# Three modulation blocks accumulated on VectorE instead of TensorE, and two blocks moved to the NSA attention units

## The chip, the cores and the metric

One NeuronCore of a Trainium2 chip runs the whole program; the other cores are idle. The metric is the device time of one launch in microseconds (us), the median over runs. TensorE (PE in the profile) multiplies matrices, VectorE (DVE) and ScalarE (ACT) work elementwise, GpSimd is POOL, and SyncE (SP) issues the transfers from HBM into the on-chip SBUF. Each engine runs its own instructions strictly in order and waits on semaphores for the others. Matrix products land in eight banks of PSUM.

## What is computed

The reference is one layer with three mixers and a mixture of experts, followed by two layers (NSA attention, then a recurrent mixer), each with a SwiGLU feed-forward part. T = 256 tokens, D = 1024, everything in float32. The part that the change touches is the modulation: a vector times a weight matrix of 1024 x 6144, three times over, whose results shift, scale and gate the activations.

```python
def first_block(x, c, ctx, c_ctx, w_mod, b_mod, ...):
    sc = jax.nn.silu(c)
    mod_x = (sc @ w_mod[layer] + b_mod[layer]).reshape(-1, N_MOD, d)
    mod_c = (scc @ w_mod[layer][:, :n_mod_c * d] + ...)      # n_mod_c = 2
    hx = modulate(rms_norm(x, g_mix[layer]), mod_x[:, 0], mod_x[:, 1])
    ...
    x = x + mod_x[:, 2, None] * mx
    hx = modulate(rms_norm(x, g_ffn[layer]), mod_x[:, 3], mod_x[:, 4])
    x = x + mod_x[:, 5, None] * expert_choice_ffn(hx, ...)

def second_block(x, c, ada_w, ada_b, ...):
    cond = jax.nn.silu(c)
    for layer in range(DEPTH_2):
        mod = (cond @ ada_w[layer] + ada_b[layer])[:, None, :]
        sh1, sc1, g1, sh2, sc2, g2 = jnp.split(mod, 6, axis=-1)
```

## The kernel before

**One list of steps.** `plan_steps` writes one list, `STEPS`, and every engine walks it in order and executes its share of each step: `("kr", 0)` is 96 matmuls on PE and two copies out of PSUM on ACT, `("rot", "kr", 0)` one matmul on PE and three operations on DVE. So the place of a step in the list fixes its place in each engine's queue.

**Weights as chunks.** All weights come as 408 chunks of 128 x 2048 float32 (1 MB), in the order in which the steps use them (`CHUNKS`). SP loads them into the slots of `ring`. In the first stage there are six slots (0, 1, 2, 3, 6, 8), from `("gate", 0)` on four (0 to 3), for the experts twelve, and afterwards nine. SP loads chunk c into its slot only when the semaphore `chunk_used` says that the chunk six places earlier has been used. PE raises it: a finished step adds to `owed`, and the next plain matmul hands `owed` over (`settle`). In the first gate stage SP takes the chunks in order too, so that gate 1 queues behind gate 0.

**Split.** A projection weight is used as a pair of fp32r numbers. `("split", x)` makes it: ACT copies the chunk to an upper slot (4 or 5) as the high part (L1240), then DVE subtracts to leave the low part in the chunk's own slot (L1540). PE then does three matmuls of 256 columns for each product (`mm3`), waiting once for `lo_ready`. Each split stands in the list one projection ahead of its use.

**Modulation.** The modulation rows are nine blocks of 2048 columns, each of eight chunks `("mod", b, k)`. For a chunk PE does four matmuls (one per 32 output rows of `mods`, PSUM bank 7) of 512 columns with the vector `silu_c` as weights, accumulating over k. `("mod_row", b)` copies the rows out on ACT (L1329), and `("mod_out", b)` transposes them on PE (L622) and adds the bias on DVE (L1585, L1588). Block 0 comes first, since its results are needed by `("apply", 0)`, which normalizes the inputs and splits them (L1530, L1525 on DVE; L1224, L1226 on ACT). Blocks 1 to 5 are `fill`: seven items before the first projection (`FILL_START`), then two or one after a projection (`FILL_LONG`, `FILL_SHORT`), and one for each unit of window and neighbourhood attention (`att_s`, `att_n`, `att_t`, `att_o`). Blocks 6 to 8 are the fill of the 37 rounds of NSA units (`nsa_s`, `nsa_n`, `nsa_t`, `nsa_o`). Block 1 is first used when the mixers' output is added to x, block 2 in the norm ahead of the experts, block 3 in the norm ahead of the NSA part, blocks 4 and 5 from that part's output on.

**Order of the stages.** Block 0 and the norm; the projections kr, qr, vr, gr, kvw, qw, kn, vn, qn with retention between them; gates; window and neighbourhood attention; branches and merge; the experts; the NSA projections, compression and units; feed-forward; the recurrent mixer; feed-forward.

Of the kernel before, what the change touches and what calls it, by code (L numbers as in the profile page):

```python
# [20 lines left out]
ALU = mybir.AluOpType  # L21
# [20 lines left out]
MOD_BLOCKS, LAST_BLOCKS = 9, 6  # L42
# [6 lines left out]
FILL_START, FILL_LONG, FILL_SHORT, GATE_EVERY = 7, 2, 1, 2  # L49
# [27 lines left out]
def plan_steps():  # L77
# [10 lines left out]
    fill = blocks(1, LAST_BLOCKS)  # L88

    def take(n):  # L90
        for _ in range(min(n, len(fill))):
            s.append(fill.pop(0))

    s.append(("apply", 0))
    take(FILL_START)
# [41 lines left out]
    fill += blocks(LAST_BLOCKS, MOD_BLOCKS)  # L137
    for i in range(units + LAG + 2):
        if i < units:
            s.append(("nsa_s", i))  # L140
        take(1)
        if 0 <= i - LAG + 1 < units:
            s.append(("nsa_n", i - LAG + 1))
        if 0 <= i - LAG < units:
            s.append(("nsa_t", i - LAG))
        if 0 <= i - LAG - 1 < units and (i - LAG - 1) % 2:
            s.append(("nsa_o", (i - LAG - 1) // 2))
# [80 lines left out]
def with_splits(steps):  # L228
# [4 lines left out]
    for u in uses:  # L233
# [10 lines left out]
        before.setdefault(x, []).append(("split", u))  # L244
    return [y for x in steps for y in before.get(x, []) + [x]], place
# [89 lines left out]
def build(nc, w, small, out):  # L335
# [9 lines left out]
    with ctx:  # L345
# [63 lines left out]
        decay_in = room(9216, N_DECAY)  # L409
        rope_a, rope_b = room(15872, 2, T), room(16384, 2, T)  # L410
# [66 lines left out]
        silu_ready, mod_done, sq_x, sq_ctx = sem("silu_ready"), sem("mod_done"), sem("sq_x"), sem("sq_ctx")  # L477
        sq_ready, std_ready, h_scaled, h_ready = sem("sq_ready"), sem("std_ready"), sem("h_scaled"), sem("h_ready")
# [135 lines left out]
        def _(pe):  # L614
# [120 lines left out]
            def step_mod(blk, k):  # L735

                ck = ring[:, slot_of(CHUNK_NO[("mod", blk, k)]), :]
# [721 lines left out]
        def _(dve):  # L1459
# [117 lines left out]

            def step_mod_out(blk):
# [16 lines left out]
                elif blk == 2:  # L1595
                    link(v.scalar_tensor_tensor(mod_a[:, 1, :], mod[:, 32:40, 0], 1.0, gain_of(1), ALU.add, ALU.mult))
                elif blk in (LAST_BLOCKS - 1, MOD_BLOCKS - 1):

                    for ni in (3, 4) if blk == LAST_BLOCKS - 1 else (5, 6):
                        at = SHIFT2[ni] + 8  # L1600
                        link(v.scalar_tensor_tensor(mod_a[:, ni, :], mod2[:, at:at + 8], 1.0, gain_of(ni), ALU.add,
                                                    ALU.mult))
# [358 lines left out]
            def step_rnn_add():  # L1961
                for p in range(4):
# [3 lines left out]
                     "mod_out": step_mod_out,  # L1966
# [181 lines left out]
```

## Time and profile before

| | us |
|---|---|
| median of 3 runs (1866.33 to 1878.32) | 1867.08 |
| span of the profiled execution | 1866.7 |
| PE busy (86% of the span) | 1601.3 |
| DVE busy (44%) | 814.8 |
| ACT busy (31%) | 585.5 |
| bytes read from HBM | 435 MB, 234 GB/s over the span |

The kernel has stages with different limits. In slices 12 to 21 of the page's 40 (about 560 to 1010 us) the transfers run at 421 to 423 GB/s, which are the experts; elsewhere PE is 80 to 100% busy and the transfers run at half that rate or less. A share of busy time averages over these stages, so a change in one of them has to be read from that stage alone.

### The profile page before, as it was taken

Reading aid. Unit: us, or ns where it says so; the run is one execution under the profiler, and the core shown is the slowest. Engines: PE = TensorE matmul, PEld = TensorE weight load, DVE = VectorE, ACT = ScalarE, POOL = GpSimd, SP = SyncE. Lnnn points to the kernel's source line nnn. Section 1 sums busy time; section 2 is a strip of 40 time slices with the busy share of each in tenths; the row PEclk is TensorE's granted clock in tenths of the full one; section 3 lists DMA queues with packets and bytes.
Section 4 is the critical chain, followed back from the end, with each engine's and each line's share of the span. In section 5 each row is a group of like instructions: output and inputs, shape, how many; then the busy total and the mean of one; then the engine's idle time right before and its main releaser. Section 6 shows DMA issues by size and latency. Waiting matters only on the chain. (4 is left out here: it accounts for less than half of the span.)

```text
span 1866.7 us, 27285 instructions
## 1 busy us (share of the span) xinstructions
PE 1601.3 (86%) x11234; PEld 1176.9 (63%) x11234; DVE 814.8 (44%) x1274; ACT 585.5 (31%) x833; POOL 20.6 (1%) x21
## 2 busy tenths in 40 slices
PE   5899998999966666766667799999999989889999
PEld 1689886666941111111114787547899989779999
DVE  4433336576641101000011765455665466766553
ACT  3322135663320000000001431443433344833332
POOL 0000020000000000000000000000000000200000
PEclk9899999999977667677767896989999999989999
DMA  9665455511729999999999253752455435335550
GB/s 395 252 253 204 181 183 211 237 68 46 284 104 423 421 422 422 421 422 422 423 422 421 77 182 111 254 197 99 143 186 182 181 136 181 136 113 183 182 178 24
DMA packets 60418, 437.76 MB, mean 235 GB/s; under 512 B 6720, under 2 KB 6848, under 8 KB 7456
## 3 DMA queue, kind: packets, MB, share of 16 engines
q1 hardware_dynamic: 59328, 428.89, 58.8%
q10 hardware_dynamic: 720, 4.94, 0.6%
q0 software_dynamic: 272, 2.49, 0.4%
q8 instruction: 77, 1.26, 0.3%
q14 instruction: 21, 0.17, 0.0%
HBM read 435.25 MB, written 1.05 MB: 234 GB/s over the span
## 5 line engine op out<-in xcount | busy, mean ns | idle before, releaser
L618 PE MATMUL bank<-H_r,ring_r 128*128 128x256 f32 x3488 | 509.8, 288 | 18.5 <-DVE H_r L1525 18.5
L618 PEld LDWEIGHTS bank<-H_r,ring_r 128*128 128x128 f32 x3488 | 464.5, 196 | 24.0 <-issue 22.6
L618 PE MATMUL bank<-arena_r,ring_r 128*128 128x256 f32 x2776 | 397.6, 287 | 25.2 <-DVE ring_r L1540 22.2
L1540 DVE TENSOR_TENSOR ring_r<-ring,ring_r 128x2048 fp32r<-128x2048 f32 x136 | 314.1, 2311 | 216.4 <-ACT ring_r L1240 216.0
L618 PEld LDWEIGHTS bank<-arena_r,ring_r 128*128 128x128 f32 x2776 | 369.2, 194 | 40.2 <-issue 18.6
L1240 ACT ACTIVATE ring_r<-ring 128x2048 fp32r<-128x2048 f32 x136 | 259.6, 1909 | 218.6 <-PE bank L618 164.4
L934 PE MATMUL bank<-ring,arena 128*32 128x512 f32 x1024 | 201.8, 881 | 105.9 <-DMA ring<-in_w 104.4
L934 PEld LDWEIGHTS bank<-ring,arena 128*32 128x32 f32 x1024 | 24.6, 127 | 267.8 <-DMA ring<-in_w 259.8
L618 PE MATMUL bank<-arena 128*64 128x256 f32 (+8 forms) x664 | 172.3, 402 | 4.0 <-DVE arena L1797 2.0
L1789 DVE TENSOR_TENSOR arena<-arena,bank 64x512 f32<-64x512 f32 x16 | 11.1, 692 | 290.7 <-ACT arena L1335 290.7
L618 PEld LDWEIGHTS bank<-arena 64*128 64x128 f32 (+4 forms) x664 | 99.4, 185 | 57.5 <-issue 28.6
L1335 ACT ACTIVATE arena<-bank 64x512 f32<-64x512 f32 x16 | 9.4, 589 | 387.2 <-PE bank L934 387.2
L955 PE MATMUL bank<-ring,arena 128*32 128x256 f32 x1024 | 91.7, 514 | 21.4 <-DMA ring<-in_w 13.5
L618 PE MATMUL bank<-ring,silu_c 128*32 128x512 f32 x576 | 85.8, 685 | 25.8 <-DMA ring<-in_w 17.0
L955 PEld LDWEIGHTS bank<-ring,arena 128*32 128x32 f32 x1024 | 37.0, 141 | 71.2 <-DMA ring<-in_w 33.1
L1797 DVE COPY arena<-bank 32x256 f32 x64 | 26.9, 420 | 123.1 <-PE bank L955 122.4
L1409 ACT ACTIVATE arena<-bank 128x256 f32<-128x256 f32 x44 | 16.9, 384 | 153.7 <-PE bank L618 153.7
L618 PE MATMUL bank<-ring_r,H_r 128*128 128x256 f32 (+1 forms) x256 | 57.6, 285 | 0.0
L618 PE MATMUL bank<-ring_r 128*128 128x256 f32 (+1 forms) x304 | 56.4, 283 | 0.0
L1919 DVE TENSOR_TENSOR arena<-arena,bank 128x256 f32<-128x256 f32 x44 | 18.5, 421 | 75.7 <-ACT arena L1409 75.7
L618 PEld LDWEIGHTS bank<-ring_r 128*128 128x128 f32 x304 | 48.3, 193 | 0.0
L618 PEld LDWEIGHTS bank<-ring,silu_c 128*32 128x32 f32 x576 | 13.1, 113 | 55.1 <-DMA ring<-in_w 28.5
(233 smaller groups left out, 1274.5 us busy)
## 6 DMA issues: line engine op xcount, KB each, us to landing
ring<-in_w SPq DMA_DIRECT2D x408, 1024.0 KB, 10.4
ring<-in_bias POOLq DMA_DIRECT2D x1, 2048.0 KB, 7.8
consts<-in_consts ACTq DMA_DIRECT2D x1, 1567.0 KB, 25.2
X<-in_x ACTq DMA_DIRECT2D x1, 1024.0 KB, 10.8
arena<-in_ctx ACTq DMA_DIRECT2D x1, 1024.0 KB, 15.3
arena<-in_decay ACTq DMA_DIRECT2D x1, 1024.0 KB, 19.8
out_t<-X SPq DMA_DIRECT2D x4, 256.0 KB, 2.5
wide<-in_wide POOLq DMA_DIRECT2D x1, 256.0 KB, 9.1
```

The lines of the kernel that those rows point to most:

```text
L618: i = nc.tensor.matmul(o, lhsT, rhs, start=start, stop=stop, skip_group_check=grouped)
L934: last = mm(bank[0][32 * j:32 * j + 32, :], x_cur[:, k, :], ring[:, k, 512 * j:512 * j + 512], start=k == 0, stop=k == KT - 1)
L955: last = mm(bank[2][32 * j:32 * j + 32, 0:T], hid_t[:, k % 4, k // 4 * CAP:k // 4 * CAP + CAP], ck[:, kk, j * T:j * T + T], start=k == 0, ...
L1240: f(r(hi), lo, ACT.Copy).then_inc(hi_ready, 1)
L1335: f(silu_g[64:P, :], bank[0][0:64, :], ACT.Silu).then_inc(silu_g_ready, 1)
L1409: f(ffn_g[:, i % 2, :], b[:, 0:T], ACT.Silu).then_inc(ffn_silu, 1)
L1540: v.tensor_tensor(r(lo), lo, r(hi), ALU.subtract).then_inc(lo_ready, 1)
L1789: v.tensor_tensor(hid[64:P, :], silu_g[64:P, :], bank[0][64:P, :], ALU.mult).then_inc(hid_ready, 1)
L1797: o = v.tensor_copy(y_tok[32 * u:32 * u + 32, i, j * T:(j + 1) * T], bank[2][32 * j:32 * j + 32, 0:T])
L1919: link(v.tensor_tensor(p, ffn_g[:, i % 2, :], b[:, T:2 * T], ALU.mult))
```

## The change

Blocks 1, 2 and 3 are no longer multiplied on PE. A new step `("mod_add", b, k)` on DVE multiplies the 128 x 2048 chunk by the vector's element of each partition and adds it to `mod_acc` (2048 columns in `arena`). PE no longer reads these chunks: at `("mod", b, k)` it waits for the semaphore `mod_added`, and at k = 7 four matmuls with ones as weights sum `mod_acc` over the partitions. The chunk counts as used only after that place in PE's order. The step stands ahead of the chunk two places earlier in `CHUNKS` (`ADD_AHEAD`). `FILL_START` is gone; three items follow a long and two a short projection. Blocks 4 and 5 move to the NSA units, where each second round now takes two items.

```diff
-MOD_BLOCKS, LAST_BLOCKS = 9, 6
+MOD_BLOCKS, ADD_BLOCKS = 9, 4
-FILL_START, FILL_LONG, FILL_SHORT, GATE_EVERY = 7, 2, 1, 2
+ADD_AHEAD = 2
+
+FILL_LONG, FILL_SHORT, GATE_EVERY = 3, 2, 2
...
-    fill = blocks(1, LAST_BLOCKS)
+    fill = blocks(1, ADD_BLOCKS)
...
     s.append(("apply", 0))
-    take(FILL_START)
...
-    fill += blocks(LAST_BLOCKS, MOD_BLOCKS)
+    fill += blocks(ADD_BLOCKS, MOD_BLOCKS)
...
-        take(1)
+        take(1 + i % 2)
...
+    for c, x in enumerate(CHUNKS):
+        if x[0] == "mod" and 0 < x[1] < ADD_BLOCKS:
+            at = CHUNKS[c - ADD_AHEAD]
+            before.setdefault(("kr", 0) if at[:2] == ("mod", 0) else at, []).append(("mod_add",) + x[1:])
...
+        mod_acc = room(11264, CHUNK)
...
+        mod_added = sem("mod_added")
...
             def step_mod(blk, k):
 
+                if 0 < blk < ADD_BLOCKS:
+                    pe.wait_ge(mod_added, (blk - 1) * KT + k + 1)
+                    if k == KT - 1:
+                        begin(("mod_row", blk))
+                        for j in range(4):
+                            mm(mods[32 * j:32 * j + 32, :], ones[:, 0:32], mod_acc[:, 512 * j:512 * j + 512], True, True,
+                               mod_done if j == 3 else None)
+                    owed[0] += 1
+                    return
...
+            def step_mod_add(blk, k):
+                c = CHUNK_NO[("mod", blk, k)]
+                at = 2 * k if blk < 3 else 16 + k
+                dve.wait_ge(landed[slot_of(c)], 16 * landed_count(c))
+                if k == 0 and blk == 1:
+                    dve.wait_ge(silu_ready, 2)
+                if k == 0 and blk > 1:
+
+                    dve.wait_ge(mod_done, blk)
+                if k == 0:
+                    o = v.tensor_scalar(mod_acc, ring[:, slot_of(c), :], silu_c[:, at:at + 1], None, ALU.mult)
+                else:
+                    dve.wait_ge(mod_added, (blk - 1) * KT + k)
+                    o = v.scalar_tensor_tensor(mod_acc, ring[:, slot_of(c), :], silu_c[:, at:at + 1], mod_acc, ALU.mult,
+                                               ALU.add)
+                o.then_inc(mod_added, 1)
```

Where the new step lands shows first in VectorE's queue, from the end of `("apply", 0)` (the H_r rows) on. A row with `ring_r<-ring,ring_r` is the low half of a split. Before, six of them stand there, with one `mod_out` (L1585) between:

```order
L1525 SCALAR_TENSOR_TENSOR H_r<-H,mod,ring_r 128x256
L1540 TENSOR_TENSOR ring_r<-ring,ring_r 128x2048 x4
L1585 TENSOR_TENSOR mod<-bank,cols 128x16 x2
L1540 TENSOR_TENSOR ring_r<-ring,ring_r 128x2048 x2
L1632 COPY arena<-bank 128x2x256 x2
```

Now, at the same place (kr 1's split first; kr 0's stands ahead of `("apply", 0)`):

```order
L1541 SCALAR_TENSOR_TENSOR H_r<-H,mod,ring_r 128x256
L1556 TENSOR_TENSOR ring_r<-ring,ring_r 128x2048
L1604 TENSOR_SCALAR arena<-ring,silu_c 128x2048
L1607 SCALAR_TENSOR_TENSOR arena<-ring,silu_c,arena 128x2048 x3
L1556 TENSOR_TENSOR ring_r<-ring,ring_r 128x2048
L1607 SCALAR_TENSOR_TENSOR arena<-ring,silu_c,arena 128x2048 x3
L1556 TENSOR_TENSOR ring_r<-ring,ring_r 128x2048
L1607 SCALAR_TENSOR_TENSOR arena<-ring,silu_c,arena 128x2048
L1604 TENSOR_SCALAR arena<-ring,silu_c 128x2048
```

Four multiply-adds of 2048 columns now stand between the splits of kr 1 and qr 0, and three between those of qr 0 and qr 1. Of the latter the first two (k = 4 and 5) are waited for by PE ahead of qr 0.

On TensorE, between the last matmul of kr 1 and the first of qr 0 (with the semaphores that each waits for), two chunks of fill stood before:

```order
L618 MATMUL bank<-ring_r 128x256
L618 MATMUL bank<-ring,silu_c 32x512 [waits act_emptied,landed0]
L618 MATMUL bank<-ring,silu_c 32x512 x3
L618 MATMUL bank<-ring,silu_c 32x512 [waits landed1]
L618 MATMUL bank<-ring,silu_c 32x512 x3
L618 MATMUL bank<-arena_r,ring_r 128x256 [waits lo_ready]
```

Now nothing stands there but the wait for VectorE's sum:

```order
L625 MATMUL bank<-ring_r 128x256 x2
L625 MATMUL bank<-H_r,ring_r 128x256
L625 MATMUL bank<-ring_r 128x256
L625 MATMUL bank<-arena_r,ring_r 128x256 [waits mod_added,lo_ready]
L625 MATMUL bank<-H_r,ring_r 128x256
```

The two groups of fill are gone, and the first matmul of qr 0 waits for `mod_added` besides `lo_ready`.

The order of the chunks moves with it. Before it was mod 0 0 to mod 1 6 (numbers 0 to 14), kr 0 (15), mod 1 7 (16), kr 1 (17). Now it is mod 0 0 to 0 7 (0 to 7), kr 0 (8), mod 1 0 to 1 2 (9 to 11), kr 1 (12), mod 1 3 to 1 5 (13 to 15), qr 0 (16), mod 1 6 and 1 7 (17, 18), qr 1 (19), mod 2 0 (20), vr 0 (21), and so on to qn 1 (48) in slot 0 and gate 0 (49), in slot 0 too.

## Rows read from the trace of the kernel before

**Rows 1.** Windows of core 0: busy us (x instructions) per engine, PEclk, DMA share, GB/s

```profile
core 0: us, PE busy (x) PEld busy (x) DVE busy (x) ACT busy (x) POOL busy (x), PEclk, DMA share, GB/s
...
61.50:67.00 5.50, 5.49 (x25) 5.50 (x26) 2.29 (x1) 1.91 (x1) 0.00 (x0) 0.50 1.03 427
...
77.00:267.00 190.00, 190.00 (x1494) 169.48 (x1498) 65.86 (x65) 44.01 (x37) 7.83 (x2) 1.00 0.53 205
267.00:304.00 37.00, 29.80 (x198) 20.28 (x190) 26.36 (x23) 18.05 (x20) 1.72 (x1) 0.99 0.61 227
304.00:312.00 8.00, 7.64 (x43) 7.64 (x44) 4.15 (x8) 6.18 (x9) 0.00 (x0) 0.62 0.36 132
312.00:400.00 88.00, 87.08 (x556) 60.41 (x555) 52.55 (x112) 56.99 (x86) 0.00 (x0) 1.00 0.47 181
...
600.00:900.00 300.00, 199.28 (x1332) 42.52 (x1328) 26.69 (x60) 22.56 (x30) 0.00 (x0) 0.69 1.01 422
...
1155.00:1290.00 135.00, 129.33 (x676) 68.99 (x669) 68.54 (x179) 54.45 (x183) 0.00 (x0) 0.88 0.52 187
```

**Rows 2.** The same windows for instructions on `silu_c` alone: the modulation matmuls

```profile
61.00:267.00 206.00, 20.04 (x164) 4.02 (x168) 0.00 (x0) 0.00 (x0) 0.98 0.52 203
...
312.00:400.00 88.00, 8.52 (x64) 1.28 (x64) 0.00 (x0) 0.00 (x0) 1.00 0.47 181
1155.00:1290.00 135.00, 30.41 (x192) 3.89 (x184) 0.00 (x0) 0.00 (x0) 0.88 0.52 187
```

**Rows 3.** Timeline of PE and ACT, 49 to 63 us: start, us, instruction, [idle before <-releaser]

```profile
49.78 1.18 PE L618 MATMUL bank<-ring,silu_c 128*32 128x512 f32 x8 [2.59 <-DMA ring<-in_w]
52.27 1.93 PE L618 MATMUL bank<-ring,silu_c 128*32 128x512 f32 x8 [1.30 <-DMA ring<-in_w]
...
57.22 1.91 ACT L1240 ACTIVATE ring_r<-ring 128x2048 fp32r<-128x2048 f32 x1 [0.78 <-DMA ring<-in_w]
...
61.51 0.58 PE L618 MATMUL bank<-arena_r,ring_r 128*128 128x256 f32 x1 [4.82 <-DVE ring_r L1540]
...
62.18 1.91 ACT L1240 ACTIVATE ring_r<-ring 128x2048 fp32r<-128x2048 f32 x1 [3.05 <-DMA ring<-in_w]
```

**Rows 4.** Timeline of DVE: `("apply", 0)` first and last, splits, a scalar_tensor_tensor

```profile
44.33 0.48 DVE L1530 SCALAR_TENSOR_TENSOR H<-X,mod_a,norm_t 128x256 f32<-128x256 f32 x1
...
56.61 0.48 DVE L1525 SCALAR_TENSOR_TENSOR H_r<-H,mod,ring_r 128x256 fp32r<-128x256 f32 x1
...
59.16 2.29 DVE L1540 TENSOR_TENSOR ring_r<-ring,ring_r 128x2048 fp32r<-128x2048 f32 x1 [2.08 <-ACT ring_r L1240]
...
118.97 0.68 DVE L1614 TENSOR_TENSOR arena<-arena,consts 128x512 f32<-128x512 f32 x1
...
223.27 0.69 DVE L1648 SCALAR_TENSOR_TENSOR ring<-bank,ring 128x512 f32<-128x512 f32 x1 [1.37 <-PE bank L618]
...
315.65 0.49 DVE L1697 TENSOR_SCALAR ring<-ring,stat 128x512 f32<-128x512 f32 x1
```

**Rows 5.** Timeline: PE after vr 0, SP's load of gr 0's chunk, ACT's copy

```profile
115.28 1.92 PE L618 MATMUL bank<-ring,silu_c 128*32 128x512 f32 x16
...
116.49 2.39 SPq L538 DMA_DIRECT2D ring<-in_w  x3
...
121.30 1.92 ACT L1240 ACTIVATE ring_r<-ring 128x2048 fp32r<-128x2048 f32 x1 [15.67 <-DMA ring<-in_w]
```

**Rows 6.** Timeline of ACT: copies out of PSUM that close kr 1, kvw; DVE's closes kvw and kn 1

```profile
82.95 0.60 ACT L1258 ACTIVATE arena<-bank 128x512 f32<-128x512 f32 x1 [3.49 <-PE bank L618]
...
88.70 0.60 ACT L1258 ACTIVATE arena<-bank 128x512 f32<-128x512 f32 x1 [5.16 <-PE bank L618]
...
152.87 0.60 ACT L1266 ACTIVATE arena<-bank 128x512 f32<-128x512 f32 x1 [3.66 <-PE bank L618]
...
163.55 0.69 DVE L1637 COPY arena<-bank 128x512 f32<-128x512 f32 x1 [11.94 <-PE bank L618]
...
205.07 0.69 DVE L1641 COPY arena<-bank 128x512 f32<-128x512 f32 x1 [3.50 <-PE bank L618]
```

**Rows 7.** Timeline of PE at 304 us: the restart after a stall

```profile
304.36 0.58 PE L618 MATMUL bank<-arena_r,ring_r 128*128 128x256 f32 x1 [5.28 <-DVE ring_r L1540]
```

**Rows 8.** Timeline of PE in an NSA round

```profile
1170.89 1.06 PE L618 MATMUL bank<-ring,silu_c 128*32 128x512 f32 x8
1171.89 0.66 PE L622 MATMUL bank<-consts,arena 128*128 128x128 f32 x4
```

**Rows 9.** Waits of PE, 1155 to 1290 us: waited for, us, times, longest

```profile
PE bank L622 <- DVE arena L1903: 3.6, 2, 2.3
PE bank L618 <- DVE arena_r L1910: 1.0, 1, 1.0
```

More of the change, by code:

```diff
@@ L1596, in step_mod_out @@
                     link(v.scalar_tensor_tensor(mod_a[:, 1, :], mod[:, 32:40, 0], 1.0, gain_of(1), ALU.add, ALU.mult))
-                elif blk in (LAST_BLOCKS - 1, MOD_BLOCKS - 1):
-                    for ni in (3, 4) if blk == LAST_BLOCKS - 1 else (5, 6):
+                elif blk in (3, 5, MOD_BLOCKS - 1):
+                    for ni in {3: (3,), 5: (4,)}.get(blk, (5, 6)):
                         at = SHIFT2[ni] + 8
@@ L1965, in _ @@
             parts = {"sum_sq": step_sum_sq, "apply": step_apply, "split": step_split, "decay": step_decay,
-                     "mod_out": step_mod_out,
+                     "mod_out": step_mod_out, "mod_add": step_mod_add,
                      "rot": step_rot, "vr": values("vr", v_r), "vn": values("vn", v_n), "kvw": step_kvw, "kn": step_kn,
```

## The prediction, made before the changed kernel was run

> **What bounds the kernel now.** I read the windows first, to see which stages the change can touch. From 77 to 267 us, the stretch of the projections, PE is busy without a gap at full clock, DVE 65.9 of 190 us, the transfers at half rate [rows 1]. So PE is the bound there and a chunk of fill taken off it should count in full. In the gate stage (267 to 304) PE already idles 7 us; in the attention units to 400 it is busy 87.1 of 88; in the NSA stretch 129.3 of 135. At 600 to 900 us the transfers run at 422 GB/s and set the pace; nothing changes there, so that stage only shifts. Second, the fill itself: the modulation matmuls hold PE for 20.0 us between 61 and 267 us (164 records at eight a chunk, 20.5 chunks), 8.5 us for eight chunks up to 400, and 30.4 us for 24 chunks in the NSA units [rows 2]. Third, the start: ACT takes kr 0's chunk the moment it lands (57.22), the low part follows, PE starts at 61.51, and chunks land 2.5 us apart (49.78, 52.27) [rows 3]. Fourth, and this decides it, what happens to a weight that is loaded only when PE frees its slot: PE finishes vr 0 at 115.28, SP issues at 116.49, ACT starts on the chunk at 121.30 [rows 5]. From the freeing matmul to ACT that is 6.0 us. Then ACT needs 1.9 and DVE 2.3 before PE can start. Before, PE hides these 10.3 us behind other projections and behind fill that needs no partner.
>
> **The start.** kr 0's chunk is now the ninth instead of the sixteenth: seven times 2.5 us sooner, 57.2 - 17.5 = 39.7 us, so it no longer delays anyone. Its split stands ahead of `("apply", 0)` and pushes that by 2.3 us, to 59.2 (it ran from 44.33 to 57.0 [rows 4]). PE can follow the tiles and is left with about three quarters of kr 0 then. Half a key projection is 5.75 us (82.95 to 88.70 [rows 6]), and the restart costs 2.9 us of half clock as before (5.5 us at 0.50 [rows 1]): kr 0 ends at 59.2 - 2.9 + 11.5 + 2.9 = 70.8 instead of 61.5 + 11.5 + 2.9 = 75.9. Gain 5.
>
> **Work removed from PE up to the end of the gate stage.** 20.0 us of chunks, and three more in the gate stage that stand half in idle time: 1.5. Three sums with ones come back: four matmuls of 512 columns each, as a chunk, 1.0 us [rows 2], so 3. Sum with the start: -5 - 20 - 1.5 + 3 = -23.5.
>
> **Work added to DVE.** The multiply-add reads two tensors. No row shows it at 2048 columns. A scalar_tensor_tensor of 512 columns takes 0.69, a tensor_tensor 0.68, and the latter takes 2.29 at 2048 columns [rows 4]; I take 2.3. The lower bound, from a tensor_scalar of 512 columns (0.49), is 4 x 0.4 = 1.6. 24 x 2.3 = 55 us on DVE, which has 124 free: by its sum DVE is not the bound. The Trainium skill ("VectorE: DVE Perf Modes", the perf-mode tier table) gives tensor_scalar a faster mode on fp32 in SBUF, 1.23 us for 2048 elements; that would hold for the three first chunks alone and take 3 us off DVE.
>
> **The new loop.** PE passes a modulation chunk only after DVE has added it, DVE adds in its own order behind the splits, a split waits for a chunk, and SP loads a chunk only when PE has passed the one six places ahead. With up to three such chunks between two projections, six slots are little more than one projection deep. I walk it with: freed slot to ACT 6.0 us for the first chunk, 2.5 for each behind it (1.05 MB at 422 GB/s [rows 1]), ACT 1.9, DVE 2.3, multiply-add 2.3, half projection 5.75.
> - kr 1 runs 70.8 to 82.4. Its first matmul frees chunks 8 to 11, so 14, 15 and 16 (qr 0) are loaded: ACT at 70.8 + 6.0 + 5.0 = 81.8, low part 86.1, then the two multiply-adds that PE waits for, 90.7. PE stalls 8.3.
> - qr 0's start frees 12 to 15; qr 1 is the second to land: ACT 90.7 + 8.5 = 99.2, low part 103.5, one multiply-add 105.8. PE is done with qr 0 at about 98. Stall 7.9.
> - gr 0 waits 5.7 for low part and two multiply-adds. gr 1: gr 0 starts 146.7, gr 1's chunk is second: 155.2, 159.4, 161.8 with the add; gr 0 ends 152.4. Stall 9.4.
> - In the same way qw 1 6.3, kn 0 4.3, the last row copy 0.7. vr 0, vr 1 and kvw run 11.5 and 16.4 us (152.87 less 5.75 to 163.55 [rows 6]) and give the loop time; there it stalls little or not.
> - gate 0 has slot 0 after qn 1 itself. Its load starts when qn 1 is done, and only a 0.9 us matmul step is left to hide it: 9.5. Before, slot 0 there held a modulation chunk long passed.
>
> Sum: 8.3 + 7.9 + 5.7 + 9.4 + 6.3 + 4.3 + 0.7 + 9.5 = 52. The walk over the old order gives no stall between kr 0 and gate 0 and the end of kn 1 at 205.4; the trace has 205.07 [rows 6]. Clock: after 5.28 us of idling [rows 7] the stretch from 304 on again starts at a granted clock of half, 0.62 over 8 us [rows 1]. A restart costs up to 2.75 us; six stalls are that long, 0 to 16. Partly the slower PE only eats into the next stall; I take 10. Up to the end of the gate stage: -23.5 + 52 + 10 = +38.
>
> **Attention units.** 8.5 us of chunks and two transposing steps of 0.6 leave a stretch in which PE is 99% busy: -9.5, less if DVE and ACT (52.6 and 57.0 of 88 us) then set the pace.
>
> **NSA units.** Sixteen chunks come in, 1.0 us each from start to the next instruction [rows 8], and two transposes of 0.6: +17. They fill some of the 4.6 us that PE waits there for DVE [rows 9]. The transfers: 40 chunks x 2.5 = 100 us in some 150, still free. I take +14.
>
> **Sum.** 1866.7 + 38 - 9.5 + 14 = 1909 us (span and median of before differ by 0.4).
>
> **Rivals.**
> 1. The loads keep up (faster). This needs the chunk of the next projection to be freed at least 10.3 us before PE wants it, for the eight places above; then PE stays the bound, the stalls and the clock term vanish, and the sum is -23.5 - 9.5 + 14 = -19: 1848. For it speaks PE's 100% against DVE's 35%; against it that the slot count and order above are fixed by the code. The Trainium skill ("Perfetto Trace Analysis", Identifying the Most-Contended Engine) says to relieve the engine with the highest occupancy first, which is this rival's case. The same page (Optimization Strategy) says that a gap that repeats can mean too few buffers, which is mine.
> 2. The loop costs half (same). If the 6.0 us were 4 and the slow clock cost nothing, each of eight stalls shrinks by 2 to 3: 52 becomes about 32, and the sum 1866.7 - 23.5 + 32 - 9.5 + 14 = 1880; with multiply-adds of 1.6 the seven after the splits take 5 more off, 1875.
> 3. Worse than the walk (slower still). DVE's queue also delays the rotations and value copies, retention and the slow clock count in full (+6), the attention units do not speed up (+9.5), NSA costs 17 (+3): 1928. If, beyond this, the NSA transfers bound (40 chunks at their pace with SP waiting for slots), up to 8 more.
>
> **How the numbers follow.** About 1% is what a measurement of this kernel can tell from no change. The loop as walked has 0.70 and rival 3 0.11; both lie over 1% slower. Rival 2 has 0.12, half of it within 1% (up to 1886). Rival 1 has 0.07. So faster 0.07, same 0.06, slower 0.87. The likeliest case's own range is 1890 to 1925. The range that should hold the time is 1880 to 1930: below it stand rival 1 and part of 2, above it part of 3.
>
> **What would show it.** In the changed profile: PE idle before the first matmuls of qr 0, qr 1, gr 0, gr 1, qw 1, kn 0 and gate 0, each 4 to 10 us, released by DVE's multiply-add or its low part; PEclk at 0.5 behind them; ACT's high-part copies waiting for the transfers; PE's busy share between 77 and 300 us at 75 to 80% instead of 100. kr 0 starting before 50 us shows the start right. The multiply-add at 2.3 us shows the row used right. The modulation chunks in the NSA units at 40 x 1.0 to 1.25 us. It would be wrong if PE stays gapless through the projections, which would mean that the loads come sooner than six places behind PE, or if the attention units give back the shift.

## The result, and the profile after

The changed kernel takes 1910.5 us (median of 4 runs, 1905.7 to 1915.5) against 1866.7 us of the kernel before on the same chip: a ratio of 1.023, 95% interval 1.019 to 1.026, so it is slower by about 2%. The profiled execution has a span of 1903.9 us, 37.2 more than the 1866.7 of before. The other 6 to 7 us between the medians are spread between executions, and I explain the 37.2.

These are the windows of the changed kernel, with the columns of [rows 1]:

```profile
core 0: us, PE busy (x) PEld busy (x) DVE busy (x) ACT busy (x) POOL busy (x), PEclk, DMA share, GB/s
...
77.00:267.00 190.00, 149.44 (x1093) 139.25 (x1092) 100.31 (x78) 34.65 (x28) 0.00 (x0) 0.87 0.46 182
267.00:304.00 37.00, 25.27 (x172) 23.88 (x171) 13.96 (x8) 9.03 (x9) 9.35 (x2) 0.88 0.45 170
...
312.00:400.00 88.00, 76.59 (x480) 60.55 (x479) 58.28 (x97) 57.12 (x80) 0.00 (x0) 0.94 0.31 108
600.00:900.00 300.00, 197.69 (x1344) 43.51 (x1336) 26.66 (x60) 22.57 (x30) 0.00 (x0) 0.70 1.01 422
```

In the projections PE was busy 190 of 190 us and is now busy 149.4; DVE went from 65.9 to 100.3, the transfers from 205 to 182 GB/s. No engine is full in this stretch any more. The experts (600 to 900 us) are as before, at 422 GB/s. PE's waits from 60 to 312 us (waited for: us, times, longest) say for what it stands still:

```profile
PE bank L625 <- DVE arena L1607: 39.8, 6, 9.2
PE bank L625 <- DVE ring_r L1556: 11.7, 1, 11.7
PE bank L629 <- ACT norm_t L1345: 0.7, 1, 0.7
```

L1607 is DVE's multiply-add, L1556 the low part of a split. The same stretch of before has 12.4 us of waits, 4.8 of them the start of kr 0 and 5.3 a wait at 304 us.

I split the 37.2 us with operations on DVE that both kernels have: the second retention variance (end of the gate stage) and the first addition to X of each later part. Starts in us, before and after (the shift is cumulative, its own part is what that part of the kernel adds):

| place | before | after | shift | its own part |
|---|---|---|---|---|
| second retention variance | 288.84 | 328.00 | +39.2 | +39.2 |
| first addition of mix_out | 492.57 | 522.42 | +29.9 | attention -9.3 |
| first addition of combine | 1014.97 | 1043.66 | +28.7 | experts -1.2 |
| first addition of nsa_out | 1292.50 | 1333.37 | +40.9 | NSA +12.2 |
| last addition to X | 1863.41 | 1900.57 | +37.2 | rest -3.7 |

The experts and the rest run the same steps in both kernels; why the rest took 3.7 us less is left open.

### The profile page after: what moved, and what is told of

It reads as the page before. It is cut to its first block and busy times, and to the rows that moved or that the text cites. A ratio compares the mean times of both kernels' runs of the same rounds, so it can differ in the third digit from the quotient of the medians.

```text
span 1903.9 us, 27031 instructions
## 1 busy us (share of the span) xinstructions
PE 1577.8 (83%) x11066; PEld 1178.6 (62%) x11066; DVE 868.0 (46%) x1298; ACT 585.1 (31%) x833; POOL 20.4 (1%) x21
## 3 DMA queue, kind: packets, MB, share of 16 engines
q8 instruction: 75, 1.23, 0.3%
## 5 line engine op out<-in xcount | busy, mean ns | idle before, releaser
L625 PE MATMUL bank<-H_r,ring_r 128*128 128x256 f32 x3488 | 513.7, 289 | 18.5 <-DVE H_r L1541 18.5
L625 PE MATMUL bank<-arena_r,ring_r 128*128 128x256 f32 x2776 | 410.3, 291 | 58.1 <-DVE ring_r L1556 31.2
L625 PEld LDWEIGHTS bank<-arena_r,ring_r 128*128 128x128 f32 x2776 | 377.8, 197 | 73.5 <-issue 39.6
L1556 DVE TENSOR_TENSOR ring_r<-ring,ring_r 128x2048 fp32r<-128x2048 f32 x136 | 315.2, 2319 | 217.1 <-ACT ring_r L1256 216.7
L950 PE MATMUL bank<-ring,arena 128*32 128x512 f32 x1024 | 195.8, 858 | 108.5 <-DMA ring<-in_w 108.1
L625 PE MATMUL bank<-arena 128*64 128x256 f32 (+8 forms) x664 | 166.5, 394 | 4.0 <-DVE arena L1830 2.0
L625 PEld LDWEIGHTS bank<-arena 64*128 64x128 f32 (+4 forms) x664 | 96.7, 181 | 51.5 <-issue 23.2
L625 PE MATMUL bank<-ring,silu_c 128*32 128x512 f32 x384 | 57.2, 695 | 22.8 <-DMA ring<-in_w 12.1
L625 PE MATMUL bank<-arena,consts 128*128 128x512 f32 (+4 forms) x76 | 35.1, 765 | 34.9 <-DVE arena L1607 25.0
L1952 DVE TENSOR_TENSOR arena<-arena,bank 128x256 f32<-128x256 f32 x44 | 18.5, 421 | 74.9 <-ACT arena L1425 74.9
L1607 DVE SCALAR_TENSOR_TENSOR arena<-ring,silu_c,arena 128x2048 f32<-128x2048 f32 x21 | 49.3, 2348 | 1.6 <-DMA ring<-in_w 0.7
## 6 DMA issues: line engine op xcount, KB each, us to landing
X<-in_x ACTq DMA_DIRECT2D x1, 1024.0 KB, 10.7
```

The lines of the kernel that those rows point to most:

```text
L625: i = nc.tensor.matmul(o, lhsT, rhs, start=start, stop=stop, skip_group_check=grouped)
L950: last = mm(bank[0][32 * j:32 * j + 32, :], x_cur[:, k, :], ring[:, k, 512 * j:512 * j + 512], start=k == 0, stop=k == KT - 1)
L1556: v.tensor_tensor(r(lo), lo, r(hi), ALU.subtract).then_inc(lo_ready, 1)
L1607: o = v.scalar_tensor_tensor(mod_acc, ring[:, slot_of(c), :], silu_c[:, at:at + 1], mod_acc, ALU.mult, ALU.add)
L1952: link(v.tensor_tensor(p, ffn_g[:, i % 2, :], b[:, T:2 * T], ALU.mult))
```

## The loop, as the trace of the changed kernel shows it

Here is the stall before gr 1, from start to end. In the timeline of PE the two records at 144.08 are the rotation ahead of gr 0, which is drawn to 146.1, and I count gr 0 from there (its first record stands at 145.13, over the rotation's end); the eight records at 160.68 are the four matmuls with ones that sum block 2, and gr 1 follows them:

```profile
144.08 2.04 PE L625 MATMUL bank<-arena,consts 128*128 128x512 f32 x2 [5.00 <-DVE arena L1607]
...
160.68 1.94 PE L625 MATMUL bank<-arena,consts 128*32 128x512 f32 x8 [7.77 <-DVE arena L1607]
```

SP's loads, ACT's copy and DVE's queue in the same stretch of the timeline:

```profile
146.51 2.17 SPq L545 DMA_DIRECT2D ring<-in_w  x4
...
153.86 1.91 ACT L1256 ACTIVATE ring_r<-ring 128x2048 fp32r<-128x2048 f32 x1 [18.11 <-DMA ring<-in_w]
...
155.87 2.29 DVE L1556 TENSOR_TENSOR ring_r<-ring,ring_r 128x2048 fp32r<-128x2048 f32 x1 [7.63 <-ACT ring_r L1256]
158.08 2.34 DVE L1607 SCALAR_TENSOR_TENSOR arena<-ring,silu_c,arena 128x2048 f32<-128x2048 f32 x1
```

Read it as a chain: gr 0 starts at 146.1 and frees the slots; SP issues at 146.5; ACT has gr 1's chunk, the second to land, at 153.86 (7.7 us after the start; 8.5 in the walk); high part 1.9, low part 2.3, and then the multiply-add behind it in DVE's queue, 2.3, to 160.4. PE was done with gr 0 at 152.9. DVE itself stands idle 7.6 us in this chain, waiting for ACT, which waits for the transfer: DVE is the last link and not the bound, though its multiply-add of 2.3 us is part of the chain. The other stalls, PE's rows in order of time (qr 0, the sum and qr 1, qw 1, kn 0, mod_out 3, gate 0; gr 0 is the 5.00 above):

```profile
90.37 0.55 PE L625 MATMUL bank<-arena_r,ring_r 128*128 128x256 f32 x1 [9.22 <-DVE arena L1607]
...
105.24 1.93 PE L625 MATMUL bank<-arena,consts 128*32 128x512 f32 x8 [7.39 <-DVE arena L1607]
...
199.91 0.55 PE L625 MATMUL bank<-arena_r,ring_r 128*128 128x256 f32 x1 [5.63 <-DVE arena L1607]
...
212.06 1.19 PE L625 MATMUL bank<-arena,consts 128*128 128x256 f32 x2 [4.81 <-DVE arena L1607]
...
228.04 0.66 PE L629 MATMUL bank<-consts,norm_t 128*128 128x128 f32 x4 [0.74 <-ACT norm_t L1345]
...
302.00 0.58 PE L625 MATMUL bank<-arena_r,ring_r 128*128 128x256 f32 x1 [11.73 <-DVE ring_r L1556]
```

Every stall but the 0.74 is followed by a half clock. These windows of the changed kernel begin at six of the restarts; PEclk is the third number from the end:

```profile
90.40:93.80 3.40, 3.40 (x16) 3.40 (x17) 2.17 (x1) 0.00 (x0) 0.00 (x0) 0.50 0.44 145
105.20:111.50 6.30, 6.26 (x31) 4.63 (x32) 3.58 (x2) 1.91 (x1) 0.00 (x0) 0.55 0.50 176
144.10:148.40 4.30, 4.30 (x14) 3.27 (x15) 4.11 (x4) 0.00 (x0) 0.00 (x0) 0.50 0.20 32
160.70:165.40 4.70, 4.70 (x15) 2.01 (x16) 2.02 (x3) 1.91 (x1) 0.00 (x0) 0.50 0.31 94
...
212.10:216.60 4.50, 4.50 (x19) 4.32 (x20) 4.42 (x5) 1.92 (x1) 0.00 (x0) 0.50 0.46 126
302.00:306.00 4.00, 4.00 (x21) 4.00 (x22) 2.15 (x1) 0.00 (x0) 0.00 (x0) 0.58 0.00 0
```

Length times (1 - PEclk) is what each costs: 1.7, 2.8, 2.2, 2.4, 2.3, 1.7, and 1.5 behind qw 1 (3.6 us at 0.57): 14.5 us. The windows end a little behind the half clock where PEclk is above 0.50; PE itself ran at 0.50 for 3.1 to 5.6 us each time.

And this is what the change costs DVE, by form, 40 to 230 us (busy us, mean ns | idle before):

```profile
L1607 DVE SCALAR_TENSOR_TENSOR arena<-ring,silu_c,arena 128x2048 f32<-128x2048 f32 x21 | 49.3, 2348 | 1.6 <-DMA ring<-in_w 0.7
L1556 DVE TENSOR_TENSOR ring_r<-ring,ring_r 128x2048 fp32r<-128x2048 f32 x13 | 29.8, 2292 | 48.4 <-ACT ring_r L1256 48.3
L1604 DVE TENSOR_SCALAR arena<-ring,silu_c 128x2048 f32<-128x2048 f32 x3 | 3.9, 1285 | 4.7 <-PE bank L625 4.7
```

## The experiments

"Variance" is the start of the second retention variance: 288.84 before, 328.00 in the changed kernel. A ratio is against the kernel before on the chip of that run, where its median was 1866.0 to 1867.7 us; a time set against the changed kernel's 1910.5 us compares two chips.

### Each half of the change alone: `e1_nsa_only`, `e2_order_pe`

The first is the kernel before with blocks 4 and 5 moved to the NSA units:

```diff
-MOD_BLOCKS, LAST_BLOCKS = 9, 6
+MOD_BLOCKS, LAST_BLOCKS = 9, 4
...
-        take(1)
+        take(1 + i % 2)
```

> The kernel before with one part of the change alone: blocks 4 and 5 go to the NSA units, blocks 1 to 3 stay on PE. Theory 1 (the loop of slot, load, split and multiply-add holds PE up): without multiply-adds there is no loop; the attention stretch gives back 9.4 us as in the changed kernel, the NSA stretch costs 12.2, and gate 0's chunk now has slot 0 just behind qn 1, so PE waits about 9.5 us before gate 0, of which the eight chunks that left the gate stage's and attention's queue do not make up more than some 3: about 1867 + 6 - 9.4 + 12.2 = 1875 us, range 1868 to 1882. Theory 2 (the two moved blocks are what costs): 1895 to 1910, most of the loss of the changed kernel. Theory 3 (only VectorE's load costs): the same 1867 to 1870, since nothing is added to VectorE.

Measured: 1880.9 us, ratio 1.006 (1.004 to 1.009), span 1877.7. The variance comes at 293.97 (+5.1), the first mix_out addition at 488.88 (-3.7, so attention -8.8), the first nsa_out addition at 1305.60. Theory 1 holds for the places: PE waits 11.05 us before gate 0 (9.5 expected), since with less fill its slot is freed just ahead of it; its split also ran 5.37 us instead of 2.29, for a reason given below. The NSA part cost 18.2 instead of 12.2.

The second is the changed kernel with the multiplication back on PE:

```diff
-        if x[0] == "mod" and 0 < x[1] < ADD_BLOCKS:
+        if False:
...
-                if 0 < blk < ADD_BLOCKS:
+                if False:
```

> The changed kernel, its order of chunks and steps kept, but blocks 1 to 3 are multiplied on PE again and DVE has no multiply-add. Theory 1 (loop): the stalls of 4 to 9 us before qr 0, qr 1, gr 0, gr 1, qw 1 and kn 0 shrink to 0 to 2 us each, since the chunk after PE's projection no longer waits for two multiply-adds and PE itself has 20 us more to do meanwhile; gate 0 keeps its wait of about 10 us. The second retention variance lies about 11 us behind the kernel before instead of 39, and the time is about 1867 + 11 - 9.4 + 12.2 = 1881 us, range 1874 to 1890. Theory 2 (the new order of the chunks alone, three modulation chunks between projections, makes the stalls): they stay, and with the 20 us of PE's matmuls on top the time is 1910 or more. Theory 3 (the half clock behind any pause): about as theory 1, with one half-clock stretch, behind gate 0's wait.

Measured: 1887.7 us, ratio 1.011 (1.009 to 1.013), span 1885.9; variance 307.37 (+18.5, expected +11). PE's stalls are 3.4 before qr 0, 1.3, 1.3, 2.0, 0.7, and 10.7 before gate 0. So the multiply-adds, which take some 20 us of matmuls off PE, bring the variance 20.6 us later (307.37 to 328.00). Theory 2 falls: the long stalls before the projections need the adds. But the order alone already costs, by gate 0's stall above all, and I had put it 7 us too low.

### Load on DVE without the loop: `e3_dve_load`

As `e2_order_pe`, with 24 operations on DVE in the multiply-adds' places:

```diff
-                dve.wait_ge(landed[slot_of(c)], 16 * landed_count(c))
...
-                    o = v.tensor_scalar(mod_acc, ring[:, slot_of(c), :], silu_c[:, at:at + 1], None, ALU.mult)
+                    o = v.memset(mod_acc, 0.0)
...
-                    o = v.scalar_tensor_tensor(mod_acc, ring[:, slot_of(c), :], silu_c[:, at:at + 1], mod_acc, ALU.mult,
+                    o = v.scalar_tensor_tensor(mod_acc, mod_acc, silu_c[:, at:at + 1], mod_acc, ALU.mult,
```

> As the kernel with the changed order and blocks 1 to 3 on PE, but 24 operations of the changed kernel's kind (one fill, then sums of three 128x2048 operands in place) stand on DVE at the places of the multiply-adds; they read no chunk, wait for no transfer, and PE waits for none of them (their results are not used). Theory 1 (loop: it is PE's wait for DVE's sum, and the wait of that sum for its chunk, that close the loop): only the delay of the splits queued behind them is left, 2.3 to 4.7 us at places where the split's chunk is already there, so 0 to 12 us over the kernel without them: 1881 to 1895. Theory 2 (DVE's added work is the cost): 1905 to 1915, as the changed kernel, plus the 20 us of PE's own matmuls where these are not hidden, to 1930.

Measured: 1893.5 us, ratio 1.013 (1.009 to 1.016), span 1889.8; variance 305.94, which is 1.4 us earlier than without the load. The first operation of each eight is a fill, the others are sums of the same size as the multiply-adds (2.35 us), and PE waits for none. The window of the projections in `e2_order_pe`:

```profile
77.00:267.00 190.00, 180.93 (x1399) 158.49 (x1397) 62.65 (x64) 38.02 (x32) 0.54 (x1) 0.98 0.48 190
```

and with the load, in `e3_dve_load`:

```profile
77.00:267.00 190.00, 182.65 (x1423) 159.95 (x1422) 106.69 (x84) 38.03 (x32) 0.54 (x1) 0.99 0.50 196
```

DVE carries 44 us more, even more than in the changed kernel, and PE loses nothing. At the first combine addition it is still 1.1 us ahead; its NSA part, 700 us behind the added work, then takes 8.1 us more (295.9 instead of 287.8), the rest 3.1 less, and the span ends up 3.9 longer. DVE's load is ruled out as the cause of the stalls before the variance.

### The size of the multiply-add: `e4_tiny_add`

The 21 multiply-adds of this kernel leave out 2040 of their 2048 columns, so its result is not the layer's; only its time is used.

```diff
-                    o = v.scalar_tensor_tensor(mod_acc, ring[:, slot_of(c), :], silu_c[:, at:at + 1], mod_acc, ALU.mult,
+                    o = v.scalar_tensor_tensor(mod_acc[:, 0:8], ring[:, slot_of(c), 0:8], silu_c[:, at:at + 1], mod_acc[:, 0:8], ALU.mult,
```

> The changed kernel, whose 21 multiply-adds take 8 of the 2048 columns (the rest of these sums is left out), so each costs about 0.1 to 0.2 us instead of 2.35; order, waits and transfers are the same. Theory 1 (loop): the multiply-adds are only the last link; freed slot to ACT 6.0, ACT 1.9, DVE's low part 2.3 and the second or third landing at 2.5 us stay. Each stall loses what DVE's adds had on it, about 2.3 to 4.6 us where two adds stand behind a split: stalls about 4.0, 7.3, 1.4, 7.3, 4.1, 2.1, 0.7 and 9.5, sum 36 instead of 52, and with fewer half-clock stretches about 20 us less than the changed kernel: 1890, range 1882 to 1898. Theory 2 (DVE's time in the adds is the whole cost): all stalls but gate 0's vanish and the time is 1860 or less. Theory 3 (slots and landings alone, adds play no part): 1905 to 1912.

Measured: 1895.1 us, ratio 1.015 (1.013 to 1.016), span 1892.7; variance 308.95, 19.1 us earlier than in the changed kernel. The time fell by 15.4 where 20 was expected, since the NSA part took 6.0 us more (295.7 against 289.7). PE's waits, 60 to 312 us:

```profile
PE bank L625 <- DVE arena L1607: 22.9, 6, 6.6
PE bank L625 <- DVE ring_r L1556: 14.4, 2, 11.7
PE bank L629 <- ACT norm_t L1345: 0.7, 1, 0.7
```

At 0.22 us an add, PE still waits six times for L1607: what it waits for there is the landing of the chunk. Of the 14.4 us, 2.65 are a wait at a later gate, which in the changed kernel falls behind 312 us; the stalls up to gate 0 are 5.2, 4.7, 1.1, 6.6, 3.6, 1.8, 0.7 and 11.7, together 35.4 where 36 was expected (one by one they are off by up to 2.6). And `e2_order_pe`, with all these matmuls on PE, has its variance at 307.37, 1.6 us sooner: in this order and with six slots, 20 us of matmuls off PE are worth nothing even when the adds cost next to nothing, since PE waits for the landings instead.

### The slots: `e5_gate_slot`, `e7_seven`

```diff
-RING_USE = [(0, (0, 1, 2, 3, 6, 8), (4, 5)), (FIRST_GATE, (0, 1, 2, 3), (4, 5)), (FIRST_EXPERT, tuple(range(SLOTS)), ()),
+RING_USE = [(0, (0, 1, 2, 3, 6, 8), (4, 5)), (FIRST_GATE, (1, 2, 3, 0), (4, 5)), (FIRST_EXPERT, tuple(range(SLOTS)), ()),
```

> The changed kernel with one line changed: the four slots of the gate stage are taken up in the order in which PE frees them (1, 2, 3, 0), so that gate 0's chunk no longer waits for qn 1, the projection just before it. Theory 1 (loop; gate 0's stall is a slot that comes free too late): the 11.7 us stall before gate 0 goes, nothing else does, and gates 1 and 2 find their chunks there; with the half clock behind it about 12 us less than the changed kernel: 1898, range 1892 to 1903. Theory 2 (bias sum on POOL and the split on DVE hold gate 0 up, not the slot): 1908 to 1912, no change.

Measured: 1899.9 us, ratio 1.018 (1.016 to 1.020), span 1898.4; variance 321.65 (-6.4), last addition to X -5.5. The wait before gate 0 is gone, as theory 1 has it: gate 0 starts at 290.92 with no idle time. But a wait of 4.35 us comes up before gate 1, whose split on DVE takes 9.51 us instead of 2.29. The first and third row are PE's, the second is DVE's:

```profile
290.92 0.47 PE L625 MATMUL bank<-arena_r,ring_r 128*128 128x256 f32 x1
...
293.53 9.51 DVE L1556 TENSOR_TENSOR ring_r<-ring,ring_r 128x2048 fp32r<-128x2048 f32 x1 [5.19 <-ACT ring_r L1256]
...
303.09 0.58 PE L625 MATMUL bank<-arena_r,ring_r 128*128 128x256 f32 x1 [4.35 <-DVE ring_r L1556]
```

So only half of the 12 comes at the variance (the median fell by 10.6). Why this split is slow is told below.

The seventh slot (`turned` gives the slots in the order in which they come free, without those named last):

```diff
+SEVEN = (0, 1, 2, 3, 6, 8, 11)
+FIRST_SIX = CHUNK_NO[next(x for x in _STEPS[_STEPS.index(("ret_s", 0, 0)):] if x in CHUNK_NO)]
+SIX = turned(SEVEN, FIRST_SIX, (11,))
+RING_USE = [(0, SEVEN, (4, 5)), (FIRST_SIX, SIX, (4, 5)), (FIRST_GATE, turned(SIX, FIRST_GATE - FIRST_SIX, (6, 8)), (4, 5)),
...
+        decay_t = [room(11264 + 1024 * i, 4, T) for i in range(2)]
```

> The changed kernel with a seventh ring slot up to the retention scores (slot 11, which is otherwise used only from there on; the scratch tile of the decay masks moves into the arena for that), and the slots behind taken up in the order in which they come free. Adds, order and waits are the changed kernel's. Theory 1 (loop; six slots are one projection deep): every load is asked for one chunk earlier, 1 to 6 us sooner; stalls before the projections 29 us together instead of 42, none before gate 0: about 32 us less than the changed kernel, 1878, range 1870 to 1890. Theory 2 (adds on DVE alone set the pace, slots do not): only gate 0's 12 us, 1898. Theory 3 (none of both): 1905 to 1912.

Measured: 1882.8 us, ratio 1.009 (1.007 to 1.011), span 1877.8; variance 300.27 (-27.7; 32 expected in the time, which fell by 27.7 too). PE's waits for the multiply-add are 23.2 us instead of 39.8, with the adds, their places and their length unchanged. Gate 0 has no wait, and gate 1 has one of 4.3 us behind a split of 9.48 us. Of the 27.7, some 6 are the gate slots of `e5_gate_slot`, which this kernel turns too.

### The place of the adds: `e6_ahead3`

```diff
-ADD_AHEAD = 2
+ADD_AHEAD = 3
```

> The changed kernel with one number changed: DVE's multiply-adds stand three chunks ahead of their place instead of two, so that the low part of the next projection no longer stands behind two adds whose chunk lands after its own, and more adds are done while PE works. Theory 1 (loop): each stall before a projection loses one multiply-add and its landing, 2.3 to 5 us, stalls together about 35 instead of 52 us, with fewer half-clock stretches: about 27 us less than the changed kernel, 1884, range 1876 to 1895. Theory 2 (the slots alone set the pace, where DVE takes its adds plays no part): 1905 to 1912. Theory 3 (DVE's load): 1905 to 1912 as well, since its work is the same.

Measured: 1888.0 us, ratio 1.012 (1.010 to 1.014), span 1884.5; variance 307.04 (-21.0). Half the loss goes by one number. PE's waits up to gate 0 are 33.3 us together (35 expected), gate 0's 11.6 among them; the rows hold 2.65 more of a later gate. Only 11.2 us are for the multiply-add now:

```profile
PE bank L625 <- DVE ring_r L1556: 24.0, 6, 11.6
PE bank L625 <- DVE arena L1607: 11.2, 3, 6.8
PE bank L629 <- ACT norm_t L1345: 0.7, 1, 0.7
```

### A version against both, and an unexpected stall: `e8_best7`, `e9_bias_dve`

Seven slots, adds three ahead, and only as much per projection as the loop bears:

```diff
-MOD_BLOCKS, ADD_BLOCKS = 9, 4
+MOD_BLOCKS, ADDS, LAST_BLOCKS = 9, (1, 2), 6
-FILL_LONG, FILL_SHORT, GATE_EVERY = 3, 2, 2
+FILL_START, FILL_LONG, FILL_SHORT, GATE_EVERY = 0, 2, 1, 2
```

> A version made to beat both: seven slots as above; only blocks 1 and 2 are added on DVE, three chunks ahead; two modulation chunks behind a long projection and one behind a short one, as before the change, none ahead of kr 0; blocks 4 and 5 stay ahead of the NSA units. Theory 1 (loop): with fewer adds between two projections and a slot more, PE does not wait between kr 0 and the second retention variance; 16 chunks of 1.0 us less on PE, two sums of 1.0 back, kr 0 6 us sooner, no wait before gate 0; against that 16 chunks instead of 8 in the attention units (+8). By this it lies 10 us below the kernel before: 1857, range 1850 to 1868. Theory 2 (DVE's load costs whatever the slots): 1875 to 1895. Theory 3 (PE is not the bound in the projections anyway): 1865 to 1870.

Measured: 1869.5 us, ratio 1.002 (1.000 to 1.004), span 1866.5: just outside the range of theory 1 (1850 to 1868), and its 1857 is missed by 12. In the projections it holds all the same: between kr 0 and gate 1 PE doesn't wait at all, and the variance comes at 274.61, 14.2 us sooner than before. But attention takes 218.9 us instead of 203.7: 8 for the eight chunks more, and one stall of 7.4 us at 396.9. And gate 1's split, for which PE waits 3.8 us, has this row on DVE and, beside it, this one on POOL:

```profile
245.10 10.13 DVE L1572 TENSOR_TENSOR ring_r<-ring,ring_r 128x2048 fp32r<-128x2048 f32 x1 [6.38 <-ACT ring_r L1272]
...
244.13 8.95 POOL L625 TENSOR_TENSOR ring<-ring,consts 128x4096 f32<-128x4096 f32 x1 [10.10 <-DMA ring<-in_bias]
```

The same split takes 2.29 us elsewhere. POOL ends at 253.08; 2.29 more is 255.4, and DVE ends at 255.23: as if DVE did nothing while POOL adds, and then all of its work. So I moved POOL's sum to DVE, behind the split:

```diff
-            nc.gpsimd.tensor_tensor(flat_bias, flat_bias, mask, ALU.add).then_inc(bias_ready, 1)
+            def step_na_bias():
...
+                v.tensor_tensor(flat_bias, flat_bias, mask, ALU.add).then_inc(bias_ready, 1)
```

> The version with seven slots and two added blocks, with one change: the bias mask is added by DVE (behind the split of gate 1) instead of POOL. In the run before, the split of gate 1 on DVE took 10.13 us from 245.10, beside POOL's sum from 244.13 to 253.08, where it takes 2.29 elsewhere, and PE waited 3.8 us for it. Theory 1 (DVE's split does not run while POOL's sum does: 253.08 + 2.29 is its end): the split takes 2.3 again, the sum 4 x 1.2 = 4.6 to 9 us on DVE in its idle time, PE's wait before gate 1 goes: 2 to 4 us less, 1862 to 1865. Theory 2 (the split was slow for another reason, its transfer or its place): the split still takes 8 to 10 us, and the time is the same or more.

Measured: 1862.7 us, ratio 0.997 (0.995 to 0.999), span 1861.7. DVE's rows now:

```profile
244.13 2.29 DVE L1566 TENSOR_TENSOR ring_r<-ring,ring_r 128x2048 fp32r<-128x2048 f32 x1 [6.38 <-ACT ring_r L1266]
246.34 4.42 DVE L1605 TENSOR_TENSOR ring<-ring,consts 128x4096 f32<-128x4096 f32 x1
```

The sum takes half as long as on POOL, the wait is gone, and the variance is 6.4 us earlier. By the Trainium skill ("SBUF — State Buffer", "SBUF: two separate sides") DVE and GpSimd share a pair of ports as an exclusive lock, held for a whole instruction, also against a DVE operation with two inputs from SBUF; the trace agrees. In ten of the kernels here a split meets POOL's sum, and each time it ends 2.15 to 2.16 us behind it. The first such pair was in the trace of before, unread:

```profile
265.89 4.98 DVE L1540 TENSOR_TENSOR ring_r<-ring,ring_r 128x2048 fp32r<-128x2048 f32 x1 [8.86 <-ACT ring_r L1240]
...
259.71 9.01 POOL L602 TENSOR_TENSOR ring<-ring,consts 128x4096 f32<-128x4096 f32 x1 [7.38 <-DMA ring<-in_bias]
```

### Everything together: `e10_all`, `e11_split5`, `e12_fill5`

`e10_all` is `e9_bias_dve` with blocks 4 and 5 in the NSA units and two splits moved up:

```diff
+        x = {("gate", 2): ("ret_var", 0), ("gate", 3): ("ret_var", 1)}.get(x, x)
         before.setdefault(x, []).append(("split", u))
```

> As the last one, and blocks 4 and 5 go to the NSA units as in the changed kernel, and the splits of gates 3 and 4 stand ahead of the retention variances instead of behind them (their waits held PE 2.3 and 3.8 us). Theory 1 (loop, and its causes add up): second retention variance 14 us before that of the kernel before, as with seven slots, 4 to 8 us of PE's waits in the gate stage less, attention -9.4, NSA +13: about 1850, range 1845 to 1858. Theory 2 (the moved blocks or the queue of DVE give it back): 1862 to 1872.

Measured: 1850.6 us, ratio 0.991 (0.988 to 0.994), span 1849.9. PE doesn't wait from kr 0 to 281 us; the projections' window is as full as in the kernel before, with DVE at 102.8 us, more than in the changed kernel:

```profile
77.00:267.00 190.00, 190.00 (x1467) 173.30 (x1466) 102.83 (x82) 51.33 (x46) 0.54 (x1) 1.00 0.57 223
```

One wait is left up to 312 us, at the start of the attention units (waits of PE):

```profile
PE bank L640 <- DVE ring L1747: 12.2, 1, 12.2
```

DVE and ACT set that wait together. DVE works on the second variance and the scores of the first units until 284.6, and then stands idle 6.2 us until ACT has copied the next gate's chunk; the first unit's normalisation stands behind that split:

```profile
290.78 2.29 DVE L1567 TENSOR_TENSOR ring_r<-ring,ring_r 128x2048 fp32r<-128x2048 f32 x1 [6.16 <-ACT ring_r L1267]
```

The last two kernels work on it. `e11_split5` only adds `("gate", 4): ("att_s", 0)` to that table; `e12_fill5` starts from `e10_all` too, with `LAST_BLOCKS = 5`, one item in each NSA round and `("gate", 4): ("att_s", 3)` instead:

> The last version, with the split of gate 5 moved ahead of the first attention scores. In the run before, PE had finished gate 4 at 281 us and waited 12.25 us, to 293.9, for the first unit's normalised probabilities, which stood on DVE behind this split, and the split on ACT behind three units' exponentials (ACT idle from 273.9 to 281.7). Theory 1 (the queue of DVE and ACT there sets the end): the wait is 7 to 9 us, since the split's 2.3 us on DVE still stand ahead of the scores but no longer wait for ACT: 3 to 5 us less, 1846. Theory 2 (the attention units are bound by DVE and ACT behind it in any case): the gain is given back within the units, 1850 to 1852.

> As the version before last, but block 4 goes to the attention units and only block 5 to the NSA units, and the split of gate 5 stands behind the first unit's normalisation. Theory 1 (PE's 12 us wait at the start of the attention units is room for fill): of the eight chunks three lie in the wait and cost nothing, five cost 1.05 us each, NSA gives back 6 to 7 us for eight chunks less: 1848, range 1843 to 1853. Theory 2 (the four slots of this stage make a chunk between two gates late, as when sixteen chunks stood there and one wait of 7.5 us came up at 390): 1850 to 1858.

Measured: 1848.9 us, ratio 0.992 (0.990 to 0.994), span 1844.0; and 1845.1 us, ratio 0.990 (0.987 to 0.994), span 1841.9. In `e11_split5` the wait is 5.6 instead of 12.2, and the first mix_out addition comes 4.8 us sooner (465.26 to 460.50), the first combine addition 4.6 (984.88 to 980.27), and the span is 5.9 shorter: in the profiled executions the gain stays, against theory 2, while the medians are only 1.7 apart. In `e12_fill5` the waits are 4.3 and 6.5. The intervals of the three overlap; that they beat both kernels is shown, their order among themselves isn't.

## Why the prediction was right, point by point

**Start.** Predicted: kr 0 ends at 70.8, 5 us sooner. ACT's copy that closes it stands at 69.68, against 76.0 before: 6.3. kr 0 starts at 47.70, before the 50 that I had named as the sign.

**Multiply-add.** Taken 2.3 us from the tensor_tensor of [rows 4]; 2.348 measured. The bound of 1.6 is out for it. For the three first chunks the bound was too high: 1.285, near the 1.23 us that the Trainium skill ("VectorE: DVE Perf Modes", the perf-mode tier table) gives.

**Stalls.** Predicted and measured, in order: qr 0 8.3 and 9.2; qr 1 7.9 and 7.4; gr 0 5.7 and 5.0; gr 1 9.4 and 7.8; qw 1 6.3 and 5.6; kn 0 4.3 and 4.8; the row copy 0.7 and 0.7; gate 0 9.5 and 11.7. Sum 52 and 52.3. In the row of qr 1 I let qr 0 end at about 98, 7.3 us behind its start, where half a projection is 5.75; the trace has 7.5 (90.37 to 97.85), of which 1.7 are half clock. So that row already holds clock loss that the clock term counts again. The walk's constants came from one place, the freed slot to ACT of [rows 5]. That the walk is the mechanism, and not only its sum, is shown by three runs that changed a constant of it each: the length of an add (stalls 35.4, 36 expected), its place (33.3, 35 expected), the number of slots (waits for adds 23.2, 29 expected; this run also turned the gate slots). Gate 0 is the one row whose size was right for an incomplete reason. The late slot decides, since with the slots turned gate 0 has no wait at all (`e5_gate_slot`). But its split also ran into POOL's sum (POOL 290.98 to 299.79, the split 295.79 to 302.0) and took 6.2 us instead of 2.3. Without that the wait would have been about 8 us, an estimate from these rows, where the walk had 9.5.

**Clock.** I took 10 us and it is 14.5: seven half-clock stretches, those behind the waits of 4.8 and 5.0 us among them, close to the 16 of the third rival. The whole up to the variance, -6.3 - 18.5 (20 + 1.5 less the sums' 3) + 52.3 + 14.5 = +42, against +39.2 measured; 1.1 of the difference is a wait of before (to 270.93) that the sum leaves out, and the terms are good to some 2 us together.

**Attention** -9.5 predicted, -9.3 measured. **NSA** +14 and +12.2. This hit is partly luck: ten profiled kernels ran the same 1676 PE records between the two additions in 287.8 to 295.9 us, with a mean granted clock of 0.92 to 0.89 and PE's idle time always 22 to 25 us. With the same list the part costs 10 to 18 us more than before's 277.5. The 40 chunks of modulation take 44.7 us of PE there, 1.12 each (1.0 to 1.25 forecast). Why the clock differs between the executions is left open.

**The sum.** 1909 forecast; the sum starts from the span of before, and the changed kernel's span is 1903.9, its median 1910.5. So the mechanism and most of its sizes are right, but that the number meets the median within 2 us is luck: the start, the clock and the NSA part are off by 1.3, 4.5 and 1.8 us, and not all the same way.

**Rivals.** The first (the loads keep up) is what `e10_all` became, once the adds stood earlier, a slot was added and a block fewer was moved: the arithmetic of the relief was right, and the ring's depth decided whether it could be had. The second (half the loop) would have needed 4 us from slot to ACT or adds of 1.6 us, and a slow clock that costs nothing; none of these is there. The third named DVE's queue as a danger, and `e3_dve_load` shows it worth nothing; of its terms only the clock's came close to true.

## What to carry to other kernels

Work taken off a full engine is no gain if that engine still has to pass the place where the work's buffer is released: the helper engine then stands inside the loop of slot, load and use, and the distance from freed slot to use (here 6.0 us, 2.5 for each chunk ahead, 4.2 for the split, 2.3 for each add) has to be covered by the work between two uses. Walk that loop from four rows before writing code; it gave eight stalls to within 2.2 us. If it doesn't close, change the lead of the helper, the depth of the ring, or the amount moved per use. The lead was the easiest: one number (`ADD_AHEAD`) recovered half the loss here.

## What the runs showed of the hardware that I had not expected

- A DVE tensor_tensor on two SBUF operands makes next to no progress while POOL adds two SBUF tensors: 10.13 us instead of 2.29, ending 2.15 us behind POOL. The profile counts all of it as DVE busy, so the wait looks like work.
- The same 128x4096 sum takes 8.95 us on POOL and 4.42 us on DVE.
- A tensor_scalar on 2048 float32 columns in SBUF takes 1.285 us, little over half of the scalar_tensor_tensor's 2.348.
- After its seven waits of 4.8 to 11.7 us in the changed kernel PE ran 3.1 to 5.6 us at half clock. Behind shorter waits it differed: one of 2.65 us (to 328.14) was followed by 3.4 us of half clock, one of 1.88 us (`e9_bias_dve`, to 268.32) by none.
